# Input tiles times a diagonal of reciprocal deviations, and two squares moved to VectorE

## The reference

```python
def rms_norm(x, gain):
    xf = x.astype(jnp.float32)
    var = jnp.mean(xf * xf, axis=-1, keepdims=True)
    return (xf * lax.rsqrt(var + EPS) * gain.astype(jnp.float32)).astype(x.dtype)
...
        hn = rms_norm(x, norm_mix[layer])
        proj = jnp.einsum('bsd,dn->bsn', hn, w_in[layer]) + b_in[layer]
```

## Time and profile before

| | |
|---|---|
| time, median of three runs | 1371.01 us |
| the profiled execution: its time and its span | 1371.76 and 1369.9 us |
| PE busy | 1351.7 us |
| DVE, ACT, POOL busy | 772.7, 476.2, 491.1 us |
| last input transposition starts | 30.4 us |
| mean granted TensorE clock | 0.997 |

### The profile page before, as it was taken

One profiled execution on the slowest core, in us unless ns is written; L12 is line 12 of the kernel. 1 busy time (PEld: TensorE's weight loads), 2 busy tenths in 40 slices (PEclk: granted clock), 3 DMA queues, 4 the chain that ended last, 5 costly groups with the idle time before them and its releaser, 6 DMA issues.

```text
span 1369.9 us, 17521 instructions
## 1 busy us (share of the span) xinstructions
PE 1351.7 (99%) x6254; PEld 1168.3 (85%) x6254; DVE 772.7 (56%) x1290; ACT 476.2 (35%) x1259; POOL 491.1 (36%) x448
## 2 busy tenths in 40 slices
PE   8899999999999999999999999999999999999998
PEld 6788888888889999999999988888888788888887
DVE  6999998842646465564656653048613457234323
ACT  7254645542434343343433477211100011223100
POOL 6765434504404133140413433344057416044020
PEclk9999999999999999999999999999999999999999
DMA  6322222322202021120211233366369644221111
GB/s 240 95 85 77 75 95 78 108 94 70 73 13 85 16 87 52 47 78 16 85 39 62 70 108 96 102 209 208 123 216 413 233 136 131 85 77 54 46 47 46
DMA packets 78437, 139.49 MB, mean 102 GB/s; under 512 B 9648, under 2 KB 31888, under 8 KB 78352
## 3 DMA queue, kind: packets, MB, share of 16 engines
q1 hardware_dynamic: 44208, 62.82, 15.4%
q10 hardware_dynamic: 34144, 75.56, 15.2%
HBM read 108.84 MB, written 29.51 MB: 101 GB/s over the span
## 4 chain that ended last, share of the span: by engine, by line
PE 92%; DVE 4%; DMA 1%; ACT 1%; issue 0%; POOL 0%; POOLq 0%; DVEq 0%; ACTq 0%
PE bank L1146 29%; PE bank L1150 28%; PE bank L1151 28%; PE bank L1269 2%; PE bank L1289 2%; PE bank L1258 2%; DMA g_in<-gate_dram 1%; PE bank L1278 1%; DVE qkn L983 1%; DVE qks L993 1%; DVE qkr L994 1%; DVE xc L887 1%; DVE qkr L992 1%; PE bank L1380 1%; PE bank L1187 0%
## 5 line engine op out<-in xcount | busy, mean ns | idle before, releaser
L464 POOL TENSOR_TENSOR ring<-raw,ring 128x512 fp32r<-128x512 f32 x221 | 312.1, 1412 | 815.3 <-PE bank L1151 758.4
L1146 PE MATMUL bank<-hn_hi,ring 128*128 128x512 f32 x640 | 252.4, 394 | 1.2 <-DVE hn_lo L831 1.2
L1150 PE MATMUL bank<-hn_lo,ring 128*128 128x512 f32 x640 | 249.8, 390 | 0.0
L1151 PE MATMUL bank<-hn_hi,ring 128*128 128x512 f32 x640 | 249.7, 390 | 0.0
L1146 PE MATMUL bank<-ring,hn_hi 128*128 128x512 f32 x576 | 244.1, 424 | 0.2 <-POOL ring L464 0.2
L1150 PE MATMUL bank<-ring,hn_hi 128*128 128x512 f32 x576 | 229.5, 399 | 0.0
L1151 PE MATMUL bank<-ring,hn_lo 128*128 128x512 f32 x576 | 229.5, 398 | 0.0
L468 POOL TENSOR_SCALAR ring<-raw 128x512 fp32r<-128x512 f32 x221 | 185.3, 838 | 7.9 <-DMA raw<-in_w_rnn_s 7.9
L1150 PEld LDWEIGHTS bank<-ring,hn_hi 128*128 128x128 f32 x576 | 160.1, 278 | 7.0
L1151 PEld LDWEIGHTS bank<-ring,hn_lo 128*128 128x128 f32 x576 | 159.0, 276 | 7.7
L1146 PEld LDWEIGHTS bank<-ring,hn_hi 128*128 128x128 f32 x576 | 158.4, 275 | 7.5 <-POOL ring L464 0.6
(11 more groups left out here) (174 smaller groups left out, 2071.6 us busy)
## 6 DMA issues: line engine op xcount, KB each, us to landing
raw<-in_w_tail_s SPq DMA_DIRECT2D x104, 256.0 KB, 2.8
g_in<-gate_dram ACTq DMA_DIRECT2D x48, 256.0 KB, 3.0
raw<-in_w_rnn_s SPq DMA_DIRECT2D x45, 256.0 KB, 2.7
raw<-in_w_qkv_s SPq DMA_DIRECT2D x48, 192.0 KB, 2.5
gate_dram<-g_out ACTq DMA_DIRECT2D x32, 256.0 KB, 2.0
raw<-in_w_qkv_s SPq DMA_DIRECT2D x48, 128.0 KB, 2.2
o_dram<-o_buf ACTq DMA_DIRECT2D x24, 256.0 KB, 2.0
o_in<-o_dram ACTq DMA_DIRECT2D x12, 512.0 KB, 4.1
```

What stands on the lines that cost most here:

```text
L464: nc.gpsimd.tensor_tensor(ring[:, ring_slot(p), 1], raw[:, p % RAW], ring[:, ring_slot(p), 0].bitcast(F32), ALU.subtract).then_inc(w_ready, 1)
L1146: ins = T.matmul(out, lhs[0], rhs[0], start=first, stop=False)
L1150: T.matmul(out, lhs[0], rhs[1], start=False, stop=False)
L1151: return T.matmul(out, lhs[1], rhs[0], start=False, stop=last)
```

## The change

Three things. (1) The sums of squares of tiles 1 and 3 are formed on DVE, with a multiply-and-reduce over the tile by itself, ahead of the reciprocals of tiles 0 and 2; ACT waits for them and takes the root. (2) x is not scaled. DVE scales the identity by the reciprocals (a diagonal of 128x128 for each tile), and PE forms a product of the raw block with that diagonal, which transposes and scales at once; it is an ordinary f32 matmul in place of `T.transpose`. (3) ident moves ahead of tiles 2 and 3 in SP's queue and has its own semaphore, for which PE and DVE wait.

```diff
+SQ_VECTOR = (1, 3)
...
+        x_junk_v = at("x_junk_v", [P, D], F32, X + 36864)
+        diag = at("diag", [P, NT, P], F32, X + 40960)
...
-            for t in range(4):
+            def load_x(t):
                 sp.dma_start(x_nat[:, t], a["x"][t * P:(t + 1) * P, :]).then_inc(x_in[t], 16)
-            for dst, src in ((ident, "ident"), (gain_mix, "gain_mix")):
-                sp.dma_start(dst[:], a[src]).then_inc(consts_in, 16)
+
+            load_x(0)
+            load_x(1)
+            sp.dma_start(ident[:], a["ident"]).then_inc(ident_in, 16)
+            load_x(2)
+            load_x(3)
+            sp.dma_start(gain_mix[:], a["gain_mix"]).then_inc(consts_in, 16)
...
-                    act.wait_ge(x_in[i], 16)
-                    act_link(nc.scalar.activation(x_junk[:], x_nat[:, i], ACT.Square, accum_out=ssq_x[:, i:i + 1]))
+                    if i in SQ_VECTOR:
+                        act.wait_ge(x_sq, SQ_VECTOR.index(i) + 1)
+                    else:
+                        act.wait_ge(x_in[i], 16)
+                        act_link(nc.scalar.activation(x_junk[:], x_nat[:, i], ACT.Square, accum_out=ssq_x[:, i:i + 1]))
...
+                    if i + 1 in SQ_VECTOR:
+                        dve.wait_ge(x_in[i + 1], 16)
+                        if i + 1 > SQ_VECTOR[0]:
+                            dve.wait_ge(x_sq, SQ_VECTOR.index(i + 1))
+                        V.tensor_tensor_reduce(out=x_junk_v[:], in0=x_nat[:, i + 1], in1=x_nat[:, i + 1], scale=1.0,
+                                               scalar=0.0, op0=ALU.mult, op1=ALU.add,
+                                               accum_out=ssq_x[:, i + 1:i + 2]).then_inc(x_sq, 1)
+                    if i == 0:
+                        dve.wait_ge(ident_in, 16)
                     dve.wait_ge(x_std, i + 1)
                     link(V.reciprocal(rstd_x[:, i:i + 1], std_x[:, i:i + 1]))
-                    V.tensor_scalar(x_nat[:, i], x_nat[:, i], rstd_x[:, i:i + 1], None, ALU.mult).then_inc(x_scaled, 1)
+                    V.tensor_scalar(diag[:, i], ident[:], rstd_x[:, i:i + 1], None, ALU.mult).then_inc(diag_set, 1)
...
-                        pe.wait_ge(x_scaled, 4 * h + t + 1)
-                    ins = T.transpose(start_bank(n)[:, t * P:(t + 1) * P],
-                                      x_nat[:, 4 * h + t, k * P:(k + 1) * P], ident[:])
+                        pe.wait_ge(diag_set, 4 * h + t + 1)
+                    ins = T.matmul(start_bank(n)[:, t * P:(t + 1) * P], x_nat[:, 4 * h + t, k * P:(k + 1) * P],
+                                   diag[:, 4 * h + t], start=True, stop=True)
...
-            pe.wait_ge(consts_in, 32)
+            pe.wait_ge(ident_in, 16)
```

More of the change, by code:

```diff
@@ L309, in build_layer @@
         warm_set = sem("warm_set")
+        ident_in = sem("ident_in")
+        x_sq = sem("x_sq")
         x_std = sem("x_std")
-        x_scaled = sem("x_scaled")
+        diag_set = sem("diag_set")
         xT_done = sem("xT_done")
@@ L436, in _ @@
             for t in range(4, NT):
-                sp.dma_start(x_nat[:, t], a["x"][t * P:(t + 1) * P, :]).then_inc(x_in[t], 16)
+                load_x(t)
             for dst, src in ((bias_in, "bias_in"), (chan, "chan")):
@@ L502, in _ @@
                     if i == 0:
-                        act.wait_ge(consts_in, 32)
+                        act.wait_ge(consts_in, 16)
                     h, k = divmod(i, KD)
```

## The result

The changed kernel takes 1376.43 us (median of seven runs, 1376.1 to 1377.47); the kernel before, in the same rounds, 1371.66. The ratio is 1.0033, 95% interval 1.0024 to 1.0043: slower by 0.33%, or 4.8 us, clear of the 0.2% that can be told from nothing. Forecast were +2.2 us, counted as no change, and a range from -0.6 to +5.2 us around the 1371.0 of before. The sign of the sum was right, its size was half. As a time, 1376.43 lies 0.2 above the upper end of 1376.2, because the kernel before ran at 1371.66 in these rounds; the difference of 4.8 lies within, near the end. Two executions far off the rest, 1487.67 us of the kernel before and 3479.61 us of the kernel before with the long pause, are in none of the ratios. The profiled execution has a span of 1374.6, 4.7 more than before, so its trace shows the whole difference.

A forecast was written before the change was run, and what follows sets the result against it. PE, busy 1351.7 of 1369.9 us, was taken to bound the kernel. Terms -0.5 - 1.65 + 4.5 - 0.17 = +2.2 us on 1371.0 gave 1373.2, counted as no change; range 1370.4 to 1376.2.

The forecast's parts named there:

- Price of a product: Input blocks on PE: 0.2225 us per product against 0.109 per transposition; 40 between main products add 4.5 us.
- four times a transposition: Rival, input blocks on PE: a product takes 0.437 us, 0.328 more than a transposition; +14.6 us, 1385.6; chance 0.03.
- no dearer than one: Rival, long bursts on PE: a product's second record hides behind the next load; -2.8 us, 1368.2; chance 0.04.
- The start: Up to the first main product: it comes 0.5 us earlier, at 13.8 (1.0 earlier to 0.3 later).
- The squares: Opening, on DVE: each square takes 1235 ns; tile 1 from 5.75 to 7.05, tile 3 from 8.35 to 9.65.
- the collision of diag 3: Opening, on DVE: tile 3's diagonal meets POOL's L464 and is ready at 11.9, against 10.6 without meeting POOL.
- The clock: From just after the first main product: granted clock 1.00 at 14.3 to 17.6, 1.65 us back; bounds 0 and 1.65.
- The end of the stretch: Last two hn_hi: the second no longer waits for the first, -0.17 us; the last ends near 33.9 instead of 31.7.
- The chain behind it: ACT's and DVE's chain up to 48.3: unchanged, pushed as a whole; 1 us either way for meeting POOL.
- The fall behind the wait: Behind PE's wait for xc_lo: half clock, 48.40 to 51.70 before, remains with its loss of 1.65 us.
- Later waits: After the first RNN block: little PE waiting is left, so what the change does to the opening is not given back.
- a fall of the clock: Rival, at the start of L1146: the clock falls all the same; +3.9 us, 1374.9, slower; chance 0.2.

The follow-up runs named there:

- long pause: POOL waits before its piece 10 until RNN block 1's xc halves are cut too: kernel before 1372.51 us, changed kernel 1376.64 us.
- late transpositions: Changed kernel with groups 6 to 15 transposed unscaled with the identity, the first 24 blocks still products: 1371.48 us, ratio 1.0001.
- short pause: POOL waits before its piece 10 until both halves of the first xc chain are cut: kernel before 1370.32 us, changed kernel 1373.69 us.
- ten idle products: Kernel before with the short pause, plus five warming products ahead of tile 3's transpositions and five behind them: 1369.89 us, ratio 0.9984.
- the squares alone: Kernel before with squares of tiles 1 and 3 on DVE and ident third, tiles still scaled in place and transposed: 1373.72 us, ratio 1.0015.
- half of the diagonal: Changed kernel with diagonal products only for tiles 0 to 3; tiles 4 to 7 scaled in place on DVE and transposed: 1372.15 us, ratio 1.0004.
- the diagonal alone: Changed kernel with all squares back on ACT: 1375.30 us, ratio 1.0025.

## Why the prediction was right or wrong, point by point

- **Price of a product.** Predicted 0.2225 us from four records of L1289; measured 2.68 / 12 = 0.223. (The row's 0.45 for four records gives 0.225; the slip is 0.1 us in the sum.) The 40 products on the path were to cost 4.5 us; taking them out gave 4.4. This was the step that decided. The product takes 2.0 times a transposition (0.223 against 0.109), and the rivals in which it is four times a transposition, or no dearer than one, are both out.
- **The start.** Predicted 0.5 us earlier (from 1.0 earlier to 0.3 later), measured 14.50 against 14.30, 0.2 later. The step that failed is the landing of x3: I gave ident's 64 KB an eighth of a tile's time, 0.15. With ident ahead, x3 landed at 9.0 instead of 8.2, and at 9.3 with nothing else changed. I had also put at nothing that SP issues ident first: x3's own issue comes 0.47 us later (2.56 instead of 2.09). How much of the delay is this and how much is a slower transfer, no run separates. The squares and the collision of diag 3 came out as worked out, each shifted by this.
- **The clock.** Predicted 1.00 at 14.3 to 17.6 and 1.65 us back; the profile shows 1.00, so between the two profiled executions the 1.65 is real. For the medians it was less. The mean granted clock of all executions was 0.9972 in the kernel before and 0.9977 with late transpositions behind the 24 early products, on the same chip; with the short pause it was 0.9982 in the kernel before and 0.9991 in the changed one. Of 1370 us this makes 0.7 and 1.2 us, an estimate from these means. The ten idle products could not have shown so little in the time: with them the mean clock was 0.9987 instead of 0.9982 (on another chip), about 0.7 us, and two ratios differ by 0.1%, 1.4 us, without meaning anything.
- **The end of the stretch.** By my terms with the measured start: +0.2 - 1.65 + 4.5 - 0.17 = +2.9; the last hn_hi ended 34.70 - 31.66 = 3.0 later. Here the sum closes.
- **The chain behind it.** I took it as unchanged, with 1 us either way for other meetings with POOL. It grew from 14.3 to 15.3 us, the whole of that bound; PE's return is 4.0 late. The unpaused profiles show two patterns: 14.3 and 14.4 in the kernel before and with the squares alone, 15.0 to 15.5 with only ident moved, in the changed kernel, with late transpositions, with half of the diagonal and with the diagonal alone. That it is POOL is shown by the pause (8.1 us). Since the squares alone have ident third too, its place doesn't settle which pattern comes. What does, was not tried, and each kernel has one profile only.
- **The fall behind the wait** cost a little less: PE came back at 52.35 and the clock at about 55.3, 3.0 us at half clock instead of 3.4, so 0.2 back. The same product stands 4.0 us later than before at PE's return and 3.8 later once the clock is up in both.
- **Later waits.** I counted them as nothing, and for this the prediction gave no reason beyond PE's being busy. Those for qkr grew from 1.3 to 2.1 and the one for g_in from 0.9 to 1.2; the same product stands 0.6 us later behind the first and 0.3 later behind the second. With 3.0 + 1.0 - 0.2 + 0.6 + 0.3 = 4.7 this is the whole 4.7 of the span. These waits vary from 1.1 to 2.1 and from 0.6 to 2.1 over the kernels run here, without order, so they are a spread of single profiles and not shown to come from the change.
- **The class.** The chance for slower by over 0.2% was 0.39, for no change 0.56. What lifted the time over that line were two of my doubtful terms, the start (0.7) and the chain (1.0), both at the dear end, and the 0.9 of later waits that stood in no term. That the difference still fell inside the range is in part luck: the range was widened for a fall of the clock, which did not come, and other terms filled it.

## What to carry to other kernels

A transposition that also scales is not free when it becomes a true f32 product: read the price of such a product from one that the kernel already has, and count how many stand on PE's path and how many in its waits. Here 24 of the 64 stood in waits and cost nothing that can be seen, and 40 stood between main products and cost 0.11 us each. A small constant moved ahead in a full queue can push the large transfers behind it by more than its bytes (0.75 us in the mean here, against 0.15); count its issue as well. And a wait behind two engines that share a resource should be tried with one of them held back for a moment: the short pause, two lines in POOL's loop, made the kernel before 0.19% faster (1370.32 us, interval 0.10 to 0.28%), while a longer one lost it again.

## What the hardware showed that I had not expected

- 64 KB in 512-byte rows, moved in front of two 512 KB tiles, delayed the second of them by 0.75 us in the mean of the profiles (8.2 to 8.8 without, 8.9 to 9.4 with), while 64 KB take 0.15 at the tiles' own rate. It costs 0.47 us of issue on SP, and between 5.0 and 6.0 us the core moved 252 and 303 GB/s in the changed kernel where it had moved 377 and 426.
- DVE's xc chain of twelve instructions takes 8.1 us alone and 14.3 to 15.5 beside a running POOL: single instructions grow from 0.69 to 1.68 us, by up to the length of one of POOL's. POOL's own L476 grows too, from 1.3 to as much as 3.08 us beside a 1024-column step (with the long pause).
- The place at which the granted clock falls differs between profiles with the same opening (14.3 in the kernel before, 9.2 with the short pause, none in the opening with the long one, and both pauses act only much later), so a loss by half clock read from one profile is a draw and not a constant.
